# Seven-product form for nine of sixteen row quads of a column pair in an encoder layer kernel

## The reference, cut to what matters

```python
def reference(x, emb_ln_g, emb_ln_b, rel_bias, w_in, ...):
    h = layer_norm(x, emb_ln_g, emb_ln_b)
    for l in range(DEPTH):                      # DEPTH is 1
        proj = h @ w_in[l]                      # 256 x 4096 times 4096 x 22080
        q_a, kv_a, dq, dk, dv, g_mla, g_dswa, r_mla, r_dswa = jnp.split(proj, IN_OFFSETS, axis=-1)
        a = mla_attention(q_a, kv_a, q_a_norm_g[l], w_q_b[l], kv_a_norm_g[l], w_kv_b[l])
        y_mla = (a * jax.nn.silu(g_mla)) @ w_o_mla[l]
        b = dilated_mixture(dq, dk, dv, rel_bias)
        y_dswa = (b * jax.nn.silu(g_dswa)) @ w_o_dswa[l]
        merged = jax.nn.sigmoid(r_mla) * y_mla + jax.nn.sigmoid(r_dswa) * y_dswa
        h = layer_norm(DEEPNORM_ALPHA * h + merged @ w_out[l], ln_g[l], ln_b[l])
    return h
```

## Time and profile before

| | us |
|---|---|
| median of 3 runs | 2695.66 |
| lowest and highest | 2692.89 and 2696.23 |
| span of the profiled execution | 2694.9 |
| PE busy in it | 2662.6 (99%) |
| DVE busy in it | 2019.2 (75%) |
| ACT busy in it | 1286.9 (48%) |

### The profile page before, as it was taken

The page is one execution under the profiler, slowest core; times in us unless marked ns, Lnnn a source line. Parts: engine busy times, 40 slices in busy tenths (PEclk is TensorE's granted clock), DMA queues, the critical chain, the costliest instruction groups (busy, mean ns, idle before and its releaser), DMA issues.

```text
span 2694.9 us, 32634 instructions
## 1 busy us (share of the span) xinstructions
PE 2662.6 (99%) x12402; PEld 2221.2 (82%) x12402; DVE 2019.2 (75%) x1975; ACT 1286.9 (48%) x1259; POOL 128.5 (5%) x211
## 2 busy tenths in 40 slices
PE   7999999999999999999999999999999999999998
PEld 5988888888888888888888889988888888888886
DVE  7778888888888888988888867765565566656557
ACT  5444554444444454555555555554454444433333
POOL 0000000000000000000000001110010100100000
PEclk9999999999999999999999999999999999999998
DMA  6666666665666656666666664357776777776765
GB/s 206 191 212 220 207 220 208 222 217 197 227 220 214 224 186 235 216 224 218 214 208 219 220 206 140 121 166 207 243 236 182 233 222 236 244 230 222 229 217 177
DMA packets 217224, 568.59 MB, mean 211 GB/s; under 512 B 14953, under 2 KB 31701, under 8 KB 217092
## 3 DMA queue, kind: packets, MB, share of 16 engines
q1 hardware_dynamic: 198992, 506.51, 57.0%
q0 software_dynamic: 16880, 57.85, 6.9%
q10 hardware_dynamic: 1224, 2.44, 0.2%
HBM read 540.46 MB, written 26.29 MB: 210 GB/s over the span
## 4 chain that ended last, share of the span: by engine, by line
PE 91%; DVE 5%; DMA 3%; ACT 1%; issue 1%; SPq 0%; DVEq 0%; ACTq 0%
PE acc L594 13%; PE acc L596 13%; PE acc L595 13%; PE bank L614 4%; PE bank L619 4%; PE bank L618 4%; PE acc L614 4%; PE acc L618 4%; PE acc L619 4%; DMA q_raw<-in_w_in 2%; PE acc L603 2%; PE acc L601 2%; PE acc L602 2%; PE bank L656 2%; PE bank L657 2%; PE bank L653 2%
## 5 line engine op out<-in xcount | busy, mean ns | idle before, releaser
L1005 ACT ACTIVATE q_hi<-q_raw 128x2048 fp32r<-128x2048 f32 x272 | 521.4, 1917 | 649.9 <-DVE q_raw L1284 298.5
L1290 DVE TENSOR_TENSOR q_low<-q_raw,q_hi 128x2048 fp32r<-128x2048 f32 x272 | 619.3, 2287 | 158.0 <-ACT q_hi L1005 158.0
L1207 DVE TENSOR_TENSOR w_lo<-w_raw,w_hi 128x1024 fp32r<-128x1024 f32 (+2 forms) x448 | 504.5, 1139 | 298.0 <-ACT w_hi L964 294.9
L964 ACT ACTIVATE w_hi<-w_raw 128x1024 fp32r<-128x1024 f32 (+2 forms) x448 | 431.6, 983 | 302.8 <-PE acc L596 262.6
L594 PE MATMUL acc<-w_hi,oper_hi 128*128 128x512 f32 (+1 forms) x1072 | 410.0, 382 | 0.3 <-DVE w_lo L1207 0.3
L596 PE MATMUL acc<-w_hi,oper_lo 128*128 128x512 f32 (+1 forms) x1072 | 405.7, 378 | 0.0
L595 PE MATMUL acc<-w_lo,oper_hi 128*128 128x512 f32 (+1 forms) x1072 | 405.3, 378 | 0.0
L594 PEld LDWEIGHTS acc<-w_hi,oper_hi 128*128 128x128 f32 x1072 | 201.3, 188 | 37.7 <-DVE w_lo L1207 1.5
L596 PEld LDWEIGHTS acc<-w_hi,oper_lo 128*128 128x128 f32 x1072 | 201.2, 188 | 37.3
L595 PEld LDWEIGHTS acc<-w_lo,oper_hi 128*128 128x128 f32 x1072 | 201.4, 188 | 36.1
L618 PE MATMUL bank<-q_hi,oper_hi 128*128 128x512 f32 x576 | 224.1, 389 | 0.0
(11 more groups left out here) (341 smaller groups left out, 4333.8 us busy)
## 6 DMA issues: line engine op xcount, KB each, us to landing
q_raw<-in_w_in SPq DMA_DIRECT2D x256, 1024.0 KB, 4.9
w_raw<-in_w_in SPq DMA_DIRECT2D x128, 512.0 KB, 4.4
w_raw<-in_w_out SPq DMA_DIRECT2D x128, 512.0 KB, 3.8
w_raw<-in_w_o_mla SPq DMA_DIRECT2D x64, 512.0 KB, 4.7
q_raw<-in_w_in SPq DMA_DIRECT2D x32, 512.0 KB, 4.6
w_raw<-in_w_o_dswa SPq DMA_DIRECT2D x32, 512.0 KB, 4.1
w_raw<-in_w_q_b SPq DMA_DIRECT2D x32, 384.0 KB, 3.5
w_raw<-in_w_in SPq DMA_DIRECT2D x32, 288.0 KB, 3.2
```

Of the source, the lines that this page charges most:

```text
L964: act.activation(w_hi[:, n % RING, 0:w], w_raw[:, n % RING, 0:w], ACT.Copy).then_inc(w_hi_ready, 1)
L1005: act.activation(q_hi[h][:, 0:4, :], q_raw[r][:, :, :], ACT.Copy).then_inc(q_hi_ready, 1)
L1207: dve.tensor_tensor(w_lo[:, n % RING, 0:w], w_raw[:, n % RING, 0:w], w_hi[:, n % RING, 0:w].bitcast(F32), ALU.subtract).then_inc(w_lo_read ...
L1290: dve.tensor_tensor(q_low[r], q_raw[r], q_hi[h][:, 0:4, :].bitcast(F32), ALU.subtract).then_inc(q_lo_ready, 1)
```

## The change

The tuple `SEVEN` has nine quads in place of seven: 34 quads more in the 17 pairs take the seven-product form. `T_STEPS` has two entries more and stands closer: every third slot of `qa0` and of `kva0` in place of every fourth. [...] The instructions of POOL and SP are the same.

```diff
-SEVEN = tuple(range(2, QUADS - 1, 2))
+SEVEN = (2, 4, 5, 7, 8, 10, 11, 13, 14)
...
-T_STEPS = (("qa0", 6), ("qa0", 10), ("qa0", 14), ("kva0", 4), ("kva0", 8), ("kva0", 12), ("kva1", 12))
+T_STEPS = (("qa0", 5), ("qa0", 8), ("qa0", 11), ("qa0", 14), ("kva0", 3), ("kva0", 6), ("kva0", 9), ("kva0", 12), ("kva1", 12))
...
-        R_B = R_A + 32 * K
+        R_B = R_A + 40 * K
...
-        t_lo = sb("t_lo", R_A + 14 * K, [P, len(SEVEN), 4, P], F32R)
-        h_pair = sb("h_pair", R_A + 28 * K, [P, 2, SEQ])
-        t_val = sb("t_val", R_A + 30 * K, [P, 4, P])
+        t_lo = sb("t_lo", R_A + 18 * K, [P, len(SEVEN), 4, P], F32R)
+        h_pair = sb("h_pair", R_A + 36 * K, [P, 2, SEQ])
+        t_val = sb("t_val", R_A + 38 * K, [P, 4, P])
...
-        c_first = sb("c_first", R_A + 28 * K, [P, 2, CW])
+        c_first = sb("c_first", R_A + 36 * K, [P, 2, CW])
...
-    nc = bacc.Bacc("TRN2", target_bir_lowering=False, num_devices=1)
+    nc = bacc.Bacc("TRN2", target_bir_lowering=False, num_devices=1, dynamic_dma_scratch_size=8192)
```

## The result

| | before | changed |
|---|---|---|
| time, median of 4 (us) | 2695.48 (2692.89 to 2696.23) | 2706.91 (2706.52 to 2707.54) |
| ratio, with its 95% interval | | 1.0044 (1.0030 to 1.0059) |
| span of the profiled execution (us) | 2694.9 | 2705.7 |

The changed kernel is 11.4 us slower, and the two spans stand 10.8 us apart. That lies inside the range of 2685 to 2715, 12 us above the forecast of 2695. The forecast was also that there would be no change to be told from zero, with 0.2% as the least that can be told; measured is slower by 0.44%, and the interval begins at 0.30%.

The account below looks back on a forecast made before the run. It took PE, busy 99% of the span, to bound the kernel. Its terms, -23.1 + 21.1 - 7.4 + 4.4 + 4.5 = -0.5 us, gave 2695 us, range 2685 to 2715.

Parts of the forecast that it names:

- (a): PE's path: 34 quads lose three matmuls each, -23.1 us.
- (b): DVE: 4.26 us more per added quad, 15.12 against PE's 14.96 per three quads, hidden by DVE's lead from quads 0 to 3.
- (c): Quads 6, 9, 12: PE waits while sums wait for a q_sum buffer; 1.24 us a pair, +21.1 us.
- (d): Quad 5: the old stalls go, -7.4 us; instead its load can be late for its sums, +4.4 us.
- The rule for late loads: Quad 5's load is late if it lands after quad 2's end, 20.42 us behind the pair's mixed_out; +4.4 us.
- rival 1: Quad 5's load is late in every pair, 1.5 us each: +19.6, 2715 us; chance 0.14.
- rival 4: Nothing is lost in start and no load is late: 2686 us; chance 0.14.
- (e): Token steps in qa0 and kva0: three slots too tight, 0.90 us lost per step, +4.5 us in all.
- (f): Smaller scratch and moved addresses: 0 us, at most half a microsecond for each of some 150 transfers.
- Rival 2: DVE's instructions overlap less, a triple costs DVE 15.6 us: +19, 2714 us; chance 0.04.
- Rival 3: The wait for the q_sum buffer at quads 6, 9, 12 isn't felt: 2674 us; chance 0.07.

Follow-up runs that it names:

- e11: Changed kernel with spread token steps, low part ahead of sums behind quads 6, 9, 12, stores held, plus a third q_sum buffer: 2665.66 us, ratio 0.9891.
- e12: Kernel before, with POOL's stores of a pair held until the third quad of the next pair is done: 2689.30 us, ratio 0.9980.
- e7: Changed kernel with the low part of the sums made for only 128 of 1536 elements on DVE: 2703.76 us, executed once.
- e9: Changed kernel with token steps spread out, low part ahead of sums behind quads 6, 9, 12, and POOL's stores held: 2672.91 us, ratio 0.9919.
- e4: Kernel before, with nine sets of token sums at the changed kernel's slots but its own seven seven-product quads per pair: 2700.37 us, ratio 1.0018.
- e1: Changed kernel with the nine token steps spread out, every fourth slot of qa0 and kva0 and two in kva1: 2702.66 us, ratio 1.0028.
- e5: Kernel before, with only the changed kernel's scratch of 8192 bytes and buffer addresses: 2695.68 us, ratio 1.0002.
- e2: Changed kernel with DVE's low part ahead of the waiting sums behind direct quads 6, 9 and 12: 2680.89 us, ratio 0.9947.
- e10: Changed kernel with POOL's stores of a pair held until PE has done three quads of the next: 2701.56 us, ratio 1.0023.
- e8: Changed kernel with the third instruction of the sums on 128 of 512 columns: 2681.66 us, executed once.

## Why the prediction was right or wrong

- **(a), matmuls removed.** Right: 102 fewer, and the quads of a pair take 80.92 where nothing stalls (e11), against 82.28 (e12): 1.36 x 17 = 23.1.
- **(b), DVE's work.** Its size is right to the hundredth, 15.12 against 14.96. That DVE's lead would hide the difference doesn't hold with two buffers: in the changed kernel the stalls of (c) cover it (e7), and in e9, where they are gone, it costs 0.37 a pair. Only with the third buffer is it hidden (e11).
- **(c), the new wait. This is the step that failed, by its size.** Places, number and cause were as predicted: three per pair at quads 6, 9 and 12, q_low of line 1290 the releaser, DVE idle ahead of its sums. The working had 5.13 us from the start of PE's next matmul to its restart, and two pieces of it were too small. First, the sums start 0.50 us behind the start of the quad's last matmul (715.08, 715.58), not 0.39 + 0.04; the 0.04 is near what a split on ACT took the earlier trace rows, and DVE takes 0.11: each stall is 0.07 longer, 0.57 and 2 x 0.44. Second, what follows the stall was counted at PE's full pace. It runs 0.13 slower once. The earlier trace rows had it: the eight matmuls behind the old stall span 2.11, beside 1.98 in the earlier trace rows. The working took only 694.88 from that row. So a pair loses 1.45 + 0.39 = 1.84 us, not 1.24, and a quiet one is 82.77, not 82.2: +31.3 instead of +21.1. These 10.2 us are nearly the whole miss, and they turned "no change" into slower.
- **(d), the old stall and the late loads.** The old stalls went: without a late load PE has none at quad 5. e12 shows that loads beside POOL's stores were their cause (quad 4's load 7.1 us before, 4.8 there). The rule for late loads holds pair by pair: by the changed kernel's own trace the load of quad 5 lands 0.61, 0.42, 0.84, 1.26 and 1.42 us past the 20.42 in five pairs, and their intervals exceed 82.77 by 0.63, 0.40, 0.77, 1.17 and 1.33, 4.3 together. That 4.4 was predicted is luck in part: which loads are late was taken from the trace before, and it differs from one to the next. The last pair was to lose 1.5 and lost nothing to speak of (82.82), and three of these five were to lose nothing or 0.2 at most. It was neither a late load in every pair (rival 1) nor none (rival 4).
- **(e), the token steps.** Right in place and sum, by some luck in the sizes: five stalls of 0.72 to 0.76 us, each with 0.1 behind it, and a sixth of 0.2, 4.4 in all; the sum said 4.5. It had these 0.8 to 0.9 long with no restart in them, so two small errors met there. Alone they measured +4.7 (e4) and, taken back, -4.25 (e1). Of the 5.75 us by which the first mixed_out is late, 0.6 stands already at 51 us, ahead of every instruction that the change touches (PE's transposes of line 699, 50.95 and 51.56). It is a difference between executions and no cost of the change: the last of line 699's weight loads starts at 67.2 before, at 67.8 in the changed kernel, and between 66.8 and 69.4 in the profiles of the experiments.
- **(f), the scratch.** Right: ratio 1.0002 (e5). The 0 was the author's estimate, from three stores in 83 us. No run shows a transfer held up by half a microsecond, its upper bound: POOL's issue of a store lasts 0.54 us before and 0.54 in e5.

With the measured sizes, and the 0.6 of that scatter, the sum is -23.1 + 31.3 - 7.4 + 4.3 + 4.4 + 0.6 = +10.1, against 10.8 in the spans; 0.4 of the rest are intervals of 82.84 where 82.77 is the quiet one.

**Rival 2** (DVE's instructions overlap less) is out: in e9 the next instruction starts 2.20 behind a low part that lasts 2.29 (711.56, 713.76), and a triple takes 15.12, not 15.6. So the starts lie closer than the durations there too, where DVE sets the pace; in the triple only the three instructions of the sums, of which each waits for the one before, start after its end (702.52 + 1.22 = 703.74, the next at 703.77).

**Rival 3** (2674 if the wait isn't felt) was wrong for the changed kernel and describes e2: 25.0 of its 26.0 us are the 31.3 of (c) less 17 x 0.37 = 6.3, by which DVE's pace comes up behind it.

**What stays open.** Why PE's restart costs 0.13. The clock is 1.00 there, so that isn't it. The trace shows what is different: in a stream the weights of a group's first matmul are loaded (PEld) while the matmul before it runs, and behind a stall their load waits for DVE as well and starts with the matmul. First e9, where nothing waits at this place, then the changed kernel:

```profile
719.48 1.77 PEld L614 LDWEIGHTS bank<-q_low,oper_hi 128*128 128x128 f32 x8
719.71 1.98 PE L614 MATMUL bank<-q_low,oper_hi 128*128 128x512 f32 x8
```

```profile
720.51 1.68 PEld L614 LDWEIGHTS bank<-q_low,oper_hi 128*128 128x128 f32 x8 [0.70 <-DVE q_low L1290]
```

In e9 at quad 7, PE has a gap of under 0.03 us, but the weight load had to wait (both start at 710.03), and the next matmul is again 0.11 late (710.37). So the lost head start of the weight load fits every place that was read; no run varied it apart. Second, why the load of quad 5 lands after 9.8 us in some pairs and after 7.6 in others. The first mixed_out of e10, 1.6 later than the changed kernel's, is no cost of its edit: PE's wait of 2.5 us for x_sb (0.7 in the other) lies ahead of anything that differs between the two, the last of line 699's weight loads starts at 69.4 in place of 67.8, and the profiled execution was e10's slowest, 2.3 over its median.

## What to carry to other kernels

An engine that runs its list in order can hold up another though it has time to spare: when a change adds a wait, put what the bounding engine needs next ahead of the waiting instruction. One line did this here for 26 us. A stall cost the gap and the restart behind it here (0.13 us behind gaps of 0.57 and 0.44), so many short stalls cost more than their gaps; measure the restart from the group that follows an old stall. When the slack of an engine is gone (15.12 us of work against 14.96), waits that used to be free reach the end, and then a buffer more or a store issued later pays.

## What the runs showed of the hardware

- PE's first matmuls after a gap cost 0.13 us more, whether the gap is 0.57, 0.44 or 0.04 us (the changed kernel, e7, e8), and 0.11 where only the weight load had waited (e9, gap under 0.03). Smaller matmuls, of 288 columns, lost 0.1 (changed kernel: 99.10 to 99.34 behind the stall, where starts are 0.13 apart).
- DVE starts 0.11 us after the end that the trace gives for the last matmul of a quad (715.58 against 715.08 + 0.39), and PE 0.06 after DVE's (718.17 + 2.28, 720.51).
- A 1 MiB load landed after 4.9 us at the median (before and changed) or 4.7 (e10). In the same pair quad 4's load took 7.1 us beside POOL's stores (before, 674.3) and 4.8 without them (e12, 670.7); quad 5's, issued 1.8 us behind it, took 7.6 and 7.2. The longest load took 10.0 us before and 9.8 in the changed kernel; with the stores moved to another time it took 7.4 (e10), 7.8 (e12), 8.7 (e9) and 9.0 (e11).
